# Sums of squares by one product with a matrix of ones, in eleven norms of a six-layer model

## The reference

```
g = norm_gains[layer]
h = x + 0.5 * swiglu(rmsnorm_2(x, g[0]), w_ffn_gu[layer, 0], w_ffn_down[layer, 0])
mix = mixer(rmsnorm_2(h, g[1]))            # hgrn2, mlstm, swa, hgrn2
h = h + mix
h = h + 0.5 * swiglu(rmsnorm_2(h, g[2]), w_ffn_gu[layer, 1], w_ffn_down[layer, 1])
gate = sigmoid(rmsnorm_2(h, g[3]) @ w_ple_gate[layer])
x = h + gate * (p[layer] @ w_ple_proj[layer])
```

## Time and profile before

| | |
|---|---|
| median of three executions | 2469.39 us (2461.65 to 2495.33) |
| the profiled execution's own time | 2469.58 us |
| its span | 2467.5 us |
| mean granted TensorE clock | 0.997 |
| matmul records, TensorE | 20402 |
| DVE busy | 1728.4 us (70%) |
| ScalarE busy | 1321.6 us (54%) |
| GpSimd busy | 98.3 us (4%) |
| DMA | 169 GB/s over the span |

### The profile page before, as it was taken

One profiled execution on the slowest core, in us unless ns is written; L12 is line 12 of the kernel. 1 busy time (PEld: TensorE's weight loads), 2 busy tenths in 40 slices (PEclk: granted clock), 3 DMA queues, 4 the chain that ended last, 5 costly groups with the idle time before them and its releaser, 6 DMA issues.

```text
span 2467.5 us, 51688 instructions
## 1 busy us (share of the span) xinstructions
PE 2416.6 (98%) x20402; PEld 2383.2 (97%) x20402; DVE 1728.4 (70%) x2416; ACT 1321.6 (54%) x2021; POOL 98.3 (4%) x99
## 2 busy tenths in 40 slices
PE   7989989999999999999999999999999999999999
PEld 7989989999999999999999999998999999999999
DVE  7768767667866677667666676577667766877666
ACT  5746645446664455445544554467445544756444
POOL 1010010000200000000000000000000000220000
PEclk9999999999999999999999999999999999999999
DMA  7314414555446555555365555543555555435553
GB/s 259 116 52 162 130 52 164 204 195 175 139 151 205 192 185 186 194 195 179 132 203 188 172 195 185 187 148 112 201 192 172 199 192 196 163 128 180 190 197 125
DMA packets 115233, 418.85 MB, mean 170 GB/s; under 512 B 12816, under 2 KB 13968, under 8 KB 114832
## 3 DMA queue, kind: packets, MB, share of 16 engines
q1 hardware_dynamic: 114240, 413.10, 49.5%
q0 software_dynamic: 560, 2.10, 0.3%
q10 hardware_dynamic: 288, 1.57, 0.2%
HBM read 414.62 MB, written 2.10 MB: 169 GB/s over the span
## 4 chain that ended last, share of the span: by engine, by line
PE 84%; DVE 9%; ACT 4%; issue 1%; DMA 1%; POOL 0%; SPq 0%; ACTq 0%; DVEq 0%
PE ps_gu L139 16%; PE ps_gu L145 16%; PE ps_gu L140 16%; PE ps_acc L139 8%; PE ps_acc L145 8%; PE ps_acc L140 8%; DVE w_lo L99 2%; DMA w_raw<-in_w_dram 1%; PE ps_acc L2644 1%; DVE arena L1618 1%; ACT w_hi L91 1%; ACT xn_hi L205 1%; PE ps_acc L2210 1%; PE ps_sum L139 1%; PE ps_sum L367 1%
## 5 line engine op out<-in xcount | busy, mean ns | idle before, releaser
L99 DVE TENSOR_TENSOR w_lo<-w_raw,w_hi 128x1024 fp32r<-128x1024 f32 x781 | 953.5, 1227 | 391.6 <-ACT w_hi L91 384.7
L139 PE MATMUL ps_gu<-xn_hi,w_hi 128*128 128x256 f32 x3832 | 1062.4, 281 | 31.8 <-DVE w_lo L99 13.0
L140 PE MATMUL ps_gu<-xn_hi,w_lo 128*128 128x256 f32 x3832 | 1050.6, 278 | 0.0
L91 ACT ACTIVATE w_hi<-w_raw 128x1024 fp32r<-128x1024 f32 x781 | 820.5, 1056 | 375.2 <-PE ps_gu L145 273.3
L145 PE MATMUL ps_gu<-xn_lo,w_hi 128*128 128x256 f32 x3832 | 1012.6, 278 | 0.0
L139 PEld LDWEIGHTS ps_gu<-xn_hi,w_hi 128*128 128x128 f32 x3832 | 723.0, 189 | 37.4 <-DVE w_lo L99 15.4
L140 PEld LDWEIGHTS ps_gu<-xn_hi,w_lo 128*128 128x128 f32 x3832 | 723.5, 189 | 0.2
L145 PEld LDWEIGHTS ps_gu<-xn_lo,w_hi 128*128 128x128 f32 x3832 | 698.9, 188 | 0.0
L139 PE MATMUL ps_acc<-h_hi,w_hi 128*128 128x256 f32 x1496 | 415.5, 278 | 0.4 <-issue 0.2
L145 PE MATMUL ps_acc<-h_lo,w_hi 128*128 128x256 f32 x1496 | 413.6, 276 | 0.0
L140 PE MATMUL ps_acc<-h_hi,w_lo 128*128 128x256 f32 x1496 | 413.5, 276 | 0.0
(11 more groups left out here) (462 smaller groups left out, 2636.9 us busy)
## 6 DMA issues: line engine op xcount, KB each, us to landing
w_raw<-in_w_dram SPq DMA_DIRECT2D x781, 512.0 KB, 4.1
const<-in_const_dram SPq DMA_DIRECT2D x1, 1280.0 KB, 12.3
x_res<-in_x_dram SPq DMA_DIRECT2D x2, 512.0 KB, 7.7
distance_rows<-arena POOLq DMA_DIRECT2D x1, 1024.0 KB, 5.6
p_all<-distance_rows POOLq DMA_DIRECT2D x2, 512.0 KB, 7.2
p_all<-in_p_dram ACTq DMA_DIRECT2D x1, 1024.0 KB, 5.0
out_dram<-x_res SPq DMA_DIRECT2D x8, 128.0 KB, 1.9
const<-in_const_dram ACTq DMA_DIRECT2D x1, 512.0 KB, 6.4
```

What stands on the lines that cost most here:

```text
L91: act.activation(self.w_hi[:, s, :], self.w_raw[:, r, :], ACT.Copy).then_inc(self.w_hi_ready.sem, 1)
L99: dve.tensor_tensor(self.w_lo[:, s, :], self.w_raw[:, c % NR, :], self.w_hi[:, s, :], ALU.subtract)\
L139: pe.matmul(out, self.w_hi[:, s, j0:j0 + width], rhs_hi, start=start, stop=False, skip_group_check=True)
L140: pe.matmul(out, self.w_lo[:, s, j0:j0 + width], rhs_hi, start=False, stop=False, skip_group_check=True)
```

## The change

In eleven of the eighteen norms, those ahead of a feed-forward part (but the first, which has an inner norm) and those ahead of an embedding gate, the root is made in all partitions at once:

- ScalarE's squares are scaled by 1/32, so that their sum is the mean.
- The fold goes down to one tile everywhere: `fold_step` 2 and 3 replace the last step for these norms and stand in `ffn`, on DVE, behind the splits of chunks 5 and 6 of tile 0.
- TensorE makes one full 32-bit product of the 128x128 ones with the 128x256 squares (`sum_everywhere`). In `ffn` it stands where the transposes stood; in `ple` behind the low products of the first two gate tiles.
- ScalarE takes the logarithm, plus epsilon, and then the exponential of -0.5 times it (`root_everywhere`). For that it loads the set with both functions, and behind it the set of silu or sigmoid.
- The small mean, GpSimd's power, the two transposes and DVE's copy are left out in these places.

```diff
+def sum_everywhere(k, pe, n):
+    pe.wait_ge(*k("misc_free").made())
+    pe.wait_ge(*k("squares_folded").at(n))
+    pe.matmul(k.ps_sum[:, 0:S], k.ones[:, :], k.xn[:, 0, :], start=True, stop=True).then_inc(*k("mean_sq_rows").up())
+
+def root_everywhere(k, act, at):
+    act.wait_ge(*at)
+    act.activation(k.rstd[:, :], k.ps_sum[:, 0:S], ACT.Ln, bias=k.eps[:, 0:1]).then_inc(*k("root_log").up())
+    act.wait_ge(*k("root_log").made())
+    act.activation(k.rstd[:, :], k.rstd[:, :], ACT.Exp, scale=-0.5).then_inc(k("rstd_ready").sem, 1)
...
     def fold_step(self, dve, n):
-        fold_six(self.k, dve, n, self.k.xn, self.k("square_made").at(self.squares - KD + (4, 6, 6)[n]), "squares_folded")
+        k, xn, step = self.k, self.k.xn, self.k("square_step")
+        if n < 2 or self.columns:
+            fold_six(k, dve, n, xn, k("square_made").at(self.squares - KD + (4, 6, 6)[n]), "squares_folded")
+        elif n == 2:
+            dve.wait_ge(*k("square_made").at(self.squares))
+            dve.wait_ge(*step.made())
+            dve.tensor_tensor(xn[:, 0:2, :], xn[:, 0:2, :], xn[:, 6:8, :], ALU.add).then_inc(*step.up())
+        else:
+            dve.wait_ge(*step.made())
+            dve.tensor_tensor(xn[:, 0, :], xn[:, 0, :], xn[:, 1, :], ALU.add).then_inc(*k("squares_folded").up())
...
 # ffn, TensorE
-            sum_squares(k, pe)
+            if inner:
+                sum_squares(k, pe)
...
-                    if t == 1 and n == 0 and j == (KD - 1 if k.inner else 4):
+                    if t == 1 and n == 0 and j == KD - 1 and inner:
                         rstd_rows(k, pe)
+                    if t == 1 and n == 0 and j == 4 and not inner:
+                        sum_everywhere(k, pe, k.norms)
 # ffn, ScalarE
             k.hi(act, g + AHEAD, i)
             if t == 0:
+                if inner:
+                    act.preload_act_table(ACT.Silu)
+                    root_in(k, act)
+                else:
+                    act.preload_act_table_set("natural_log_exp_and_others")
+            k.hi(act, g + 1 + AHEAD, i)
+            if t == 0 and not inner:
+                root_everywhere(k, act, k("mean_sq_rows").made())
                 act.preload_act_table(ACT.Silu)
-                root_in(k, act)
-            k.hi(act, g + 1 + AHEAD, i)
 # ffn, DVE
             k.lo(dve, g + AHEAD, i)
+            if t == 0 and not inner:
+                newest.fold_step(dve, 2)
             k.lo(dve, g + 1 + AHEAD, i)
             if t == 0:
-                take_rstd(k, dve)
+                if inner:
+                    take_rstd(k, dve)
+                else:
+                    newest.fold_step(dve, 3)
                 dve.wait_ge(*k("rstd_ready").at(k.norms))
...
 # ple, TensorE
-        sum_squares(k, pe, n, summed)
         for j in range(KD):
             pe.wait_ge(*lo_at[j])
...
-        rstd_rows(k, pe, n)
+        sum_everywhere(k, pe, n)
 # ple, ScalarE
-        act.preload_act_table(ACT.Sigmoid)
+        act.preload_act_table_set("natural_log_exp_and_others")
         for j in range(3):
             k.hi(act, c0 + j + AHEAD)
-        root_in(k, act, n)
+        root_everywhere(k, act, k("mean_sq_rows").made())
+        act.preload_act_table(ACT.Sigmoid)
 # ple, DVE
-        take_rstd(k, dve, n)
         dve.wait_ge(*k("rstd_ready").at(n))
...
         if nxt:
             nxt.split_lo(dve, KD - 1)
-            nxt.fold_step(dve, 2)
```

More of the change, by code:

```diff
@@ L185, with __init__ @@
 class Norm:
-    def __init__(self, k, gain, squares=KD):
-        self.k, self.gain = k, gain
+    def __init__(self, k, gain, squares=KD, columns=True):
+        self.k, self.gain, self.columns = k, gain, columns
+        k.columns += columns
+        k.newest = self
         k("square_made").n += squares
@@ L217, in square @@
         act.wait_ge(*at)
-        act.activation(self.k.xn[:, m, :], self.k.x[:, m, :], ACT.Square).then_inc(self.k("square_made").sem, 1)
+        act.activation(self.k.xn[:, m, :], self.k.x[:, m, :], ACT.Square, scale=D ** -0.5)\
+           .then_inc(self.k("square_made").sem, 1)
     def fold(self, dve):
@@ L261, in norm @@
     block = k.block
-    t = Norm(k, gain, squares=2)
+    t = Norm(k, gain, squares=2, columns=not ahead)
     adds, at, late = k.adds, k.x_at, k.late
@@ L272, in _ @@
         for j in range(2):
-            act.activation(half(xn, j), half(x, j), ACT.Square).then_inc(squares.sem, 1)
+            act.activation(half(xn, j), half(x, j), ACT.Square, scale=D ** -0.5).then_inc(squares.sem, 1)
         for c in late[0]:
@@ L341, in turned @@
         k = self.k
-        pe.wait_ge(*k("rstd_col").at(k.norms))
+        pe.wait_ge(*k("rstd_col").at(k.columns))
         pe.wait_ge(*k("rstd_ready").at(k.norms))
@@ L355, in to_x, with sum_squares @@
                                      op0=ALU.mult, op1=ALU.mult).then_inc(*k("x_ready").up())
-def sum_squares(k, pe, n=None, summed=None):
-    n = n or k.norms
+def sum_squares(k, pe):
     pe.wait_ge(*k("misc_free").made())
-    tiles, squares = k.summed if summed is None else summed
-    pe.wait_ge(*k("squares_folded").at(n))
+    tiles, squares = k.summed
+    pe.wait_ge(*k("squares_folded").at(k.norms))
     pe.wait_ge(*squares)
@@ L371, in sum_squares, with root_in, spread_root @@
     mm.then_inc(k("sum_sq_col").sem, 1)
-def root_in(k, act, n=None):
-    n = n or k.norms
-    act.wait_ge(*k("sum_sq_col").at(n))
+def root_in(k, act):
+    act.wait_ge(*k("sum_sq_col").at(k.columns))
     if k.inner:
         act.activation(k.inner_sq[:, :], k.ps_sum[:, TT:2 * TT], ACT.Copy, scale=1.0 / D)
-    act.activation(k.mean_sq[:, :], k.ps_sum[:, 0:TT], ACT.Identity, scale=1.0 / D, bias=k.eps[:, 0:1])\
+    act.activation(k.mean_sq[:, :], k.ps_sum[:, 0:TT], ACT.Identity, bias=k.eps[:, 0:1])\
        .then_inc(k("mean_sq_col").sem, 1)
-def spread_root(k, n=None):
-    n = n or k.norms
+def spread_root(k):
     @k.block.gpsimd
     def _(pool):
-        pool.wait_ge(k("mean_sq_col").sem, n)
+        pool.wait_ge(k("mean_sq_col").sem, k.columns)
         if k.inner:
@@ L395, in _, with rstd_rows @@
         ins.then_inc(k("rstd_col").sem, 1)
-def rstd_rows(k, pe, n=None):
-    n = n or k.norms
-    pe.wait_ge(*k("rstd_col").at(n))
-    if n == 1:
+def rstd_rows(k, pe):
+    pe.wait_ge(*k("rstd_col").at(k.columns))
+    if k.norms == 1:
         pe.wait_ge(*k("constants_loaded").made())
@@ L551, in _ @@
         tiles(dve, tile)
[L553 removed]
+    if inner:
+        spread_root(k)
     k.inner = None
@@ L619, in ple @@
     proj = lambda m: k.ps_acc[:, m // 2, (m % 2) * S:(m % 2 + 1) * S]
-    n, summed = k.norms, k.summed
-    nxt = None if next_gain is None else Norm(k, next_gain)
+    n = k.norms
+    nxt = None if next_gain is None else Norm(k, next_gain, columns=False)
     xr.n += KD
@@ L747, in setup @@
     k.inner = None
-    k.norms = 0
+    k.norms = k.columns = 0
     k.s = k.sb("silu", [P, 2, S])
@@ L832, in _ @@
             half = slice(4 * j, 4 * j + 4)
-            act.activation(k.xn[:, half, :], k.x[:, half, :], ACT.Square).then_inc(squares.sem, 1)
+            act.activation(k.xn[:, half, :], k.x[:, half, :], ACT.Square, scale=D ** -0.5).then_inc(squares.sem, 1)
         for c in range(3, AHEAD):
@@ L1159, with __init__ @@
 class OutProjection:
-    def __init__(self, k, next_gain, inner=None):
-        self.k, self.next_gain, self.inner = k, next_gain, inner
+    def __init__(self, k, next_gain, inner=None, columns=True):
+        self.k, self.next_gain, self.inner, self.columns = k, next_gain, inner, columns
         self.at, self.begun, self.banks, self.left, self.c0 = {}, set(), None, [], None
@@ L1241, in finish @@
         pr.n += KD
-        nxt, inner = Norm(k, self.next_gain), self.inner
+        nxt, inner = Norm(k, self.next_gain, columns=self.columns), self.inner
         hi, lo = self.hi, self.lo
@@ L1303, in _ @@
             nxt.split_lo(dve, KD - 1)
-            fold(dve, 2)
+            if nxt.columns:
+                fold(dve, 2)
             k.lo_for(dve, c0 + KD - 1)
@@ L3907, in build @@
             k.arena.clear()
-            o_proj = OutProjection(k, gain(layer, 2))
+            o_proj = OutProjection(k, gain(layer, 2), columns=False)
             if layer % 3 == 0:
```

8 lines of the change are left out of this document (3 added, 5 removed).

## The result

The changed kernel takes 2501.53 us, median of 20 executions (2487.64 to 2528.11); the kernel before, run beside it, takes 2474.93 (2460.91 to 2495.33, also 20). The ratio is 1.011 with a 95% interval of 1.0091 to 1.013: 27 us slower, about 1.1%, which is no difference at 2%. I had forecast 2482 and at most 2496. The profiled execution of the changed kernel is one of its longest, 2525.36 us, so it stands 24 above its own median, and 55.8 above the one shown of before. The ratio leaves out the two executions above 2520 us, this one among them, as slow ones, though its granted clock, 0.995, is like that of the others.

What follows compares the result with a forecast made beforehand. TensorE, busy 98%, was taken to bound the kernel, except in most embedding gates, where DVE's chain does. Net steps 1.2 + 5.1 + 6.4 = 12.7 us on 2469.58 gave 2482; own range 2474 to 2492, 8-in-10 range 2460 to 2496.

Steps and rivals of the forecast that it cites:

- TensorE's 8.8 us saved: Less TensorE work in eleven places: 1.12 us in each A and B, 0.23 in each C; real only where TensorE bounds.
- A: Four feed-forward parts behind a mixer: first product with down weights 0.3 us later each, 1.2 in all.
- B: Three feed-forward parts behind an embedding gate: first product with down weights 1.7 us later each, 5.1 in all.
- C: Four embedding gates, the last ending the kernel: later by 2.1, 1.7, 1.9 and 0.7 us, 6.4 in all.
- The clock falls: Rival: in B's new waits TensorE's clock halves to 1.2 GHz, 1.75 us each, 12.3 more, 2495; chance 0.05.
- The dearer switch: Rival: each ScalarE table load costs a second 1.28 us; 19.5 more in all, 2502; chance 0.05.
- All hidden: Rival: TensorE's 8.8 us come out and no wait is new; 2460.8 us; chance 0.15.
- half: Rival: only A and B, or only C, cost what was priced; about 2470 us; chance 0.08.

Runs made afterwards that it cites:

- fold_first: The changed kernel with the last two folds on DVE both ahead of the split of chunk 6; 2490.76 us, ratio 1.0059 to the kernel before.
- ffn_only: The changed kernel with the new root only in the seven feed-forward parts, embedding gates as before; 2506.78 us, ratio 1.0121 to the kernel before.
- one_pair: The kernel before with one more pair of transposes behind the first down chunk of seven feed-forward parts; 2502.25 us, ratio 1.0112.
- pair_after_15: The kernel before with two extra transpose pairs in seven feed-forward parts, behind the first down chunk and 15 products later; 2471.81 us, ratio 1.0004.
- two_pairs: The kernel before with extra transpose pairs behind the first and second down chunks of seven feed-forward parts, 72 products apart; 2519.69 us, ratio 1.0174.

## Why the prediction was wrong, by its steps

**The step that failed** is a term that the sum did not have. I wrote that a product takes 0.115 us, worked out from the earlier trace rows, and further on that three chunks take 72 x 0.118, with no row beside it, and I did not ask why they differ. In the trace the 47 products behind the 0.115 are 14 at 0.118 and 33 at 0.113. I held all products outside the eleven places fixed, had for it among the bounds only "the scatter of a median", without a size, and took three executions from 2461.65 to 2495.33 for scatter of one kernel, where by the groups they are none, one and four wide parts. That term is 42 us of the profiled difference and, by the groups, about 15 of the median's. What I did price came to 14, where I had 12.7. Beside it, the base was low: I added to 2469.58, an execution with one wide part, where the median of 20 is 2474.93. So of the 19 us between 2482 and 2501.5 five are the base.

**TensorE's 8.8 us saved, and lost.** Right: in the gate the product with ones puts 0.55 us between its start and that of the second product behind it (923.74 to 924.29), 0.43 more than one product, and the chain behind it set the end in every place. Behind a stop it is 0.62 (730.78 to 731.40).

**A**, predicted +0.3: from the last product of tile 0 to the down weights 7.21 before and 7.81 after, +0.60 in each of the four. It ended 7.81 behind that product where I had 7.51: DVE's fold to TensorE is 730.78 - 730.22 = 0.56, not 0.45, and from there to the logarithm 0.71, not 0.64; the rest is hundredths. Mis-sized by 0.3, 1.2 in all.

**B**, predicted +1.7: 9.12, 8.38 and 8.39 against 7.21, 7.32 and 7.21: +1.9, +1.1, +1.2. In the first every step is within 0.2. In the others, as in the second, the load began 0.45 before TensorE's last product of tile 0 (1475.88, 1476.33), in the first 0.28 behind it (951.14, 950.86), so it held chunk 6 less. 4.2 in all, for 5.1.

**C**, predicted 2.1 + 1.7 + 1.9 + 0.7: from the last down product to the last product of the next tile 0 it takes 32.73, 33.45, 33.45 and, at the end, to TensorE's last product, 24.12, against 30.66, 31.05, 30.81 and 23.35: 2.1 + 2.4 + 2.6 + 0.8 = 7.9. In `fold_first` it is 32.69, 32.62, 32.70 and 24.12: 2.0 + 1.6 + 1.9 + 0.8 = 6.3, almost what I had. The two that are longer have the clock rival in them, next. The three sums are 2.4 + 4.2 + 7.9 = 14.5, the 14 between the floors.

**The clock falls** came true in two places. Stretches of after at the entries into the second and third B:

```profile
1468.00:1474.00 6.00, 4.85 (x28) 4.85 (x29) 5.08 (x11) 2.17 (x6) 0.00 (x0) 0.72 0.48 165
1973.00:1979.00 6.00, 5.70 (x35) 5.71 (x36) 4.51 (x10) 2.79 (x9) 0.00 (x0) 0.72 0.37 122
```

And the same place in `fold_first`:

```profile
1461.00:1467.00 6.00, 4.29 (x34) 4.10 (x35) 5.08 (x12) 2.19 (x7) 0.00 (x0) 1.00 0.57 178
```

A granted clock of 0.72 over 6 us is 3.4 us at 1.2 GHz and the rest at 2.4. Here it fell behind the waits at the end of C, not in those before the product with ones, where I had put it; in `ffn_only` it fell there, in two B. Against `fold_first` each cost 0.8, not my 1.75; TensorE was busy for 4.85 and 5.70 of these 6 us and waited for the rest.

**The dearer switch** fell. A load is 1.28, and the next instruction starts 0.02 behind it, after the exponential too (732.43 to 733.73, 925.32 to 926.61). By the Trainium skill (ScalarE: Activation LUTs, What ACT_TABLE_LOAD costs) there would be a drain of about 1380 ns beside it; no row of this case has room for it, and the floors differ by 14, not by 34.

**All hidden** and **half** fell with the steps. Of what I said would show it all is there: TensorE stops 1.09 and 2.32 before the product with ones, DVE 1.94 before the split of chunk 8, and 100 records are gone.

## What to carry to other kernels

Ahead of pricing a change, count the bottleneck's instructions in equal stretches of its busiest loops: if two stretches of the same code differ at the same clock, the engine has two rates there, and a change in the order of its row, or a short interruption of it, may change which one holds. Sort the single times as well: groups with gaps between them say that a median is a mixture, and that one profile is one draw of it. And keep the row of the engine that bounds the kernel as it is where it has a good rate, since here 5% on some 1500 products, 8 us, weighed more than any one wait that was added.

## What the runs showed of the hardware

- TensorE's 128x256 products of 128x128 weights go on at 113.3 or 118.9 ns start to start, at a granted clock of 1.00 in both, through a whole feed-forward part (up to 182 us here). Such a stretch can end without a stop: at 722.6 in the kernel before 118.9 became 113.3 with no distance over 0.13 us. The Trainium skill (TensorE: Matmul & The Clock Gate, Back-to-back issue gap) gives N / 2.4 + 2.5 for a single matmul at full clock, 109.2 ns for 256 columns, and for streams with weight loads one value each at 128 and 512 columns; the trace has neither 109.2 nor one value alone.
- A pair of transposes turned close into wide in all four A of `one_pair`, and back 15 products later in `pair_after_15`, but not back 72 products later in `two_pairs`. The kernel's own pair, 15 products behind one-column matmuls, turned the spacing in 63 of 63 places of nine profiles. A stop of 0.39 us in A left the spacing as it is without one; stops of 0.42 to 0.48 in B left it the other way in three of three; one of 0.59, the same in four places, was followed by either. What decides stays open; the same for what the B parts enter with.
